# A delta-rule mixer joined from its projection to its scan, with the memory items woven into the feed-forward part

## The chip, the cores and the metric

The kernel runs on one core of a Trainium2 chip. The metric is the device time of one execution in microseconds; the median of three executions counts. Five things work beside one another: TensorE (PE, matmuls into eight PSUM banks), VectorE (DVE), ScalarE (ACT), GpSimd (POOL, idle here) and the DMA queue that SyncE (SP) feeds. They meet only at semaphores, and each runs its own list in order.

## The reference

Three blocks follow one another on x of 256 tokens by 1024 columns, in float32. The change touches the first one's first layer:

```python
x = x + 0.5 * swiglu(rms_norm(x, ffn1_norm[l]), ffn1_w_gu[l], ffn1_w_down[l])
h = rms_norm(x, mix_norm[l]) @ a_w_in[i]
qkv, gate, b_raw, a_raw, q_mem = jnp.split(h, ...)
o_a = gated_deltanet(qkv, gate, b_raw, a_raw, a_conv[i], a_A_log[i], a_dt_bias[i], a_out_norm[i])
o_m = memory_attention(q_mem, mem_n @ w_mem_kv[l])
x = x + jnp.concatenate([o_a, o_m], axis=-1) @ w_out[l]
```

gated_deltanet: silu of a causal convolution of four taps over qkv; q and k of each of the six heads divided by their length (`l2_norm`); beta = sigmoid(b_raw); g = -exp(A_log) * softplus(a_raw + dt_bias); per chunk of 64 tokens a triangular system from beta, k k^T and the decays exp(g_cum_i - g_cum_j), solved; then a scan over four chunks with a state of 128x128 per head; an RMS norm of the output and a factor silu(gate). The memory keys and values of both layers come from the normed 256 memory rows `mem_n`.

## The kernel before

Weights come as items of up to 1 MB (128 x 2048), in the order of `self.items`, through five slots. SyncE loads an item when its slot's last user is done (`load_weights`), ScalarE rounds it (`round_weights`, L210 and, with a gain, L214), VectorE takes the rest (`split_weights`, L227, L232), at most LEAD = 3 items ahead of TensorE, and TensorE makes three matmuls for each 128x128 block (hi*hi, hi*lo, lo*hi; L257 to L259 and L850 to L853). An item of 256 columns is 48 matmuls.

Each `K.stage` is a block; without `join` the one before is closed first, so that all engines end together. The order inside is written out by hand in one function per engine. Around the change:

- `ffn` (L813), eleven steps s: item a, item b, and the down item of the step before. An object `keys` can weave foreign items into step 0 and 1; only the latent part used it.
- `project_conv` (L1192), nine items: TensorE projects two chunks of 128 columns, VectorE scales them by the row norm into `conv_pad` (L1244), splits the next item, weighs the first tap (L1258) and adds three (L1264), ScalarE takes silu (L1229). ScalarE rounds without waiting for VectorE.
- `gates_and_memory` (L3356), nine items: three gate items, beta/a, q_mem, four memory items; the memory tokens are normed, transposed and rounded meanwhile.
- `group_norm` (L1381) on q and k: squares, 24 column sums, a root, its inverse spread to rows by matmuls with diagonals, q and k multiplied.
- transposes of k and v, the gates, `softplus` (L1446), `vector_chain`, the decays and products (L1570 to L1639), each in a stage of its own.
- the inverse (L1641 to L1717), two products, the scan (L1750 to L1806), `group_norm` of the output, `attend_memory`, `project_out`. The scan runs over four chunks: products with the state (L1768), new values (L1792), state growth (L1774), state update (L1801), outputs (L1779, L1780).

## Time and profile before

| | us |
|---|---|
| median of three executions | 3055.31 |
| lowest, highest | 3053.14, 3056.57 |
| the profiled execution | 3053.95 |
| its span in the profile | 3051.8 |
| TensorE busy | 2898.2 (95%) |
| VectorE busy | 1820.7 (60%) |
| ScalarE busy | 1457.3 (48%) |
| first feed-forward part | 29 to 217 |
| projection and convolution | 217 to 278 |
| gates and memory | 278 to 339 |
| norms of q and k | 339 to 361 |
| transposes, gates, softplus, decays, products | 361 to 402 |
| inverse, two products | 402 to 456 |
| scan | 456 to 502 |
| output norm, memory attention | 502 to 534 |

A timeline row gives start, length, engine, line, tiles and, in brackets, how long the engine had been idle and whom it waited for. Rows of one line that follow each other closely are merged (x6). Matmul lengths overlap; their pace is read from starts. A matmul of plain float32 operands shows as two records, so twelve of them are "x24".

### The profile page before, as it was taken

To read this page: it belongs to the slowest core of one execution; us is meant where nothing else is said; L and a number is where in the kernel's file an instruction comes from. 1 tells how busy PE (TensorE), PEld (TensorE's weight loads), DVE (VectorE), ACT (ScalarE), POOL (GpSimd) and SP (SyncE) were. 2 spreads that over 40 slices of the span, in tenths; PEclk is the share of its full clock that TensorE was granted. 3 is DMA by queue.
4 is the path that set the end of the run, shared out by engine and by line. 5 is a ranking of instruction groups with operands and counts; after the bars stand their busy time and mean duration, and the time that the engine had idled before them with its cause. 6 is when DMAs were issued, how large, how long until landed. Compare 5 with 4: busy or idle time off the path is not lost. (4 is left out here: it accounts for less than half of the span.)

```text
span 3051.8 us, 47640 instructions
## 1 busy us (share of the span) xinstructions
PE 2898.2 (95%) x20602; PEld 2688.5 (88%) x20602; DVE 1820.7 (60%) x2487; ACT 1457.3 (48%) x1927; POOL 16.3 (1%) x21
## 2 busy tenths in 40 slices
PE   6998788999999999999999898999999999999999
PEld 6998676899998799898999897998989899999898
DVE  5567473655656665545468756456556655656655
ACT  5554311545545554434466544445454544544543
POOL 0000000000000000000000200000000000000000
PEclk9999795999999899999999999999999999999999
DMA  6654200455554255555555254555555455554553
GB/s 199 193 180 156 80 1 0 159 187 170 176 190 160 85 193 187 173 193 166 169 166 179 79 170 164 183 178 165 193 182 177 149 184 193 179 187 146 200 188 130
DMA packets 370037, 489.16 MB, mean 160 GB/s; under 512 B 15183, under 2 KB 329124, under 8 KB 369700
## 3 DMA queue, kind: packets, MB, share of 16 engines
q1 hardware_dynamic: 369232, 485.90, 48.8%
q8 instruction: 163, 2.67, 0.4%
q14 instruction: 46, 0.38, 0.0%
q10 hardware_dynamic: 596, 0.21, 0.0%
HBM read 485.02 MB, written 1.05 MB: 159 GB/s over the span
## 5 line engine op out<-in xcount | busy, mean ns | idle before, releaser
L850 PE MATMUL work<-input_hi,weights_hi 128*128 128x256 f32 x3520 | 990.7, 281 | 8.2 <-DVE weights_lo L232 6.2
L853 PE MATMUL work<-input_hi,weights_lo 128*128 128x256 f32 x3520 | 987.1, 280 | 0.0
L852 PE MATMUL work<-input_lo,weights_hi 128*128 128x256 f32 x3520 | 987.1, 280 | 0.0
L227 DVE TENSOR_TENSOR weights_lo<-weights_raw,weights_hi 128x2048 fp32r<-128x2048 f32 (+1 forms) x282 | 629.5, 2236 | 376.2 <-ACT weights_hi L210 376.0
L850 PEld LDWEIGHTS work<-input_hi,weights_hi 128*128 128x128 f32 x3520 | 666.2, 189 | 13.8 <-DVE weights_lo L232 6.6
L852 PEld LDWEIGHTS work<-input_lo,weights_hi 128*128 128x128 f32 x3520 | 666.1, 189 | 4.4
L853 PEld LDWEIGHTS work<-input_hi,weights_lo 128*128 128x128 f32 x3520 | 665.9, 189 | 0.0
L214 ACT ACTIVATE weights_hi<-weights_raw,params 128x512 fp32r<-128x512 f32 (+2 forms) x736 | 462.0, 701 | 352.1 <-DMA weights_raw<-in_ffn_w_gu 176.2
L210 ACT ACTIVATE weights_hi<-weights_raw 128x2048 fp32r<-128x2048 f32 (+1 forms) x282 | 524.5, 1865 | 168.6 <-DMA weights_raw<-in_ffn_w_up 100.3
L232 DVE SCALAR_TENSOR_TENSOR weights_lo<-weights_raw,params,weights_hi 128x512 fp32r<-128x512 f32 (+2 forms) x736 | 492.7, 733 | 174.7 <-ACT weights_hi L214 174.6
L317 PE MATMUL acc<-weights_hi,hidden_hi 128*128 128x512 f32 x880 | 349.6, 397 | 6.3 <-DVE hidden_lo L952 5.0
L319 PE MATMUL acc<-weights_hi,hidden_lo 128*128 128x512 f32 x880 | 347.9, 395 | 0.0
L318 PE MATMUL acc<-weights_lo,hidden_hi 128*128 128x512 f32 x880 | 347.7, 395 | 0.0
L257 PE MATMUL work<-input_hi,weights_hi 128*128 128x256 f32 (+1 forms) x1008 | 287.7, 285 | 14.3 <-PEq L154 8.8
L258 PE MATMUL work<-input_lo,weights_hi 128*128 128x256 f32 (+1 forms) x1008 | 282.6, 280 | 0.0
L259 PE MATMUL work<-input_hi,weights_lo 128*128 128x256 f32 (+1 forms) x1008 | 282.3, 280 | 0.0
L941 DVE TENSOR_TENSOR gate_r<-work,inverse_root 128x512 f32<-128x512 f32 x88 | 60.8, 690 | 249.2 <-PE work L853 249.2
L257 PEld LDWEIGHTS work<-input_hi,weights_hi 128*128 128x128 f32 (+1 forms) x1008 | 189.3, 188 | 17.7 <-issue 15.3
L317 PEld LDWEIGHTS acc<-weights_hi,hidden_hi 128*128 128x128 f32 x880 | 166.1, 189 | 43.7 <-issue 8.8
L319 PEld LDWEIGHTS acc<-weights_hi,hidden_lo 128*128 128x128 f32 x880 | 166.1, 189 | 38.6
L915 ACT ACTIVATE hidden_hi<-hidden 128x512 fp32r<-128x512 f32 x110 | 69.4, 631 | 266.2 <-DVE hidden L949 266.2
L318 PEld LDWEIGHTS acc<-weights_lo,hidden_hi 128*128 128x128 f32 x880 | 166.4, 189 | 33.7
(518 smaller groups left out, 3408.8 us busy)
## 6 DMA issues: line engine op xcount, KB each, us to landing
weights_raw<-in_ffn_w_gu SPq DMA_DIRECT2D x176, 512.0 KB, 4.7
weights_raw<-in_ffn_w_in SPq DMA_DIRECT2D x176, 512.0 KB, 4.7
weights_raw<-in_ffn_w_down SPq DMA_DIRECT2D x66, 1024.0 KB, 4.9
weights_raw<-in_w_in SPq DMA_DIRECT2D x44, 1024.0 KB, 5.0
weights_raw<-in_ffn_w_out SPq DMA_DIRECT2D x44, 1024.0 KB, 4.8
weights_raw<-in_a_w_in SPq DMA_DIRECT2D x29, 1024.0 KB, 5.4
...
```

The costliest lines, as they stand in the source:

```text
L210: last = self.nc.scalar.activation(self.wh[:, n % SLOTS, 0:kc * cols], raw, ACT.Copy)
L214: last = self.nc.scalar.activation(hi[:, k, :], raw[:, k * cols:(k + 1) * cols], ACT.Copy, scale=g[:, gain[1] + k:gain[1] + k + 1])
L227: last = self.nc.vector.tensor_tensor(self.wl[:, n % SLOTS, 0:kc * cols], raw, self.wh[:, n % SLOTS, 0:kc * cols].bitcast(F32), ALU.subtract)
L232: last = self.nc.vector.scalar_tensor_tensor(out=lo[:, k, :], in0=raw[:, k * cols:(k + 1) * cols], scalar=g[:, gain[1] + k:gain[1] + k + 1 ...
L257: self.nc.tensor.matmul(o, wh[:, k, ms], hi[:, k, :], start=clear, stop=False, skip_group_check=True)
L258: self.nc.tensor.matmul(o, wh[:, k, ms], lo[:, k, :], start=False, stop=False, skip_group_check=True)
L317: self.nc.tensor.matmul(o, hi[:, k, ts], wh[:, k, cols], start=(first and k == 0), stop=False, skip_group_check=True)
L318: self.nc.tensor.matmul(o, hi[:, k, ts], wl[:, k, cols], start=False, stop=False, skip_group_check=True)
L319: last = self.nc.tensor.matmul(o, lo[:, k, ts], wh[:, k, cols], start=False, stop=(end and k == kc - 1), skip_group_check=True)
L850: nc.tensor.matmul(o, wh[:, k, ms], K.hi[:, c, :], start=(c == 0 and m == 0), stop=False, skip_group_check=True)
L852: nc.tensor.matmul(o, wh[:, k, ms], K.lo[:, c, :], start=False, stop=False, skip_group_check=True)
L853: last = nc.tensor.matmul(o, wl[:, k, ms], K.hi[:, c, :], start=False, stop=(c == DC - 1), skip_group_check=True)
```

## The change

The rest of the program stays as it is.

1. The four memory items move from behind the gates into step 1 of the first feed-forward part: class `MemoryKeys` is a second `keys` object. Its DMA of the memory tokens goes out at the start, its squares and root stand behind step 0 of ScalarE (`prepare`), its transposes in the middle of step 1, its four items behind it.
2. Projection, convolution, q_mem, norms, gates, transposes, decays and products are one joined stage of eleven items: beta/a first, then k, q, v, then q_mem. The first tap is weighed by ScalarE, beta comes from an exponential, the copies of k and v out of PSUM are ScalarE's.
3. q and k are not divided by their lengths any more. The inverse length of k enters as a column factor on the decays, on beta and on the scan's columns; that of q enters as a floor column in the output norm (`group_norm` loses its bias and gets one small VectorE operation).
4. The three gate items are projected inside the scan, half an item before and half behind the state growth of chunks 0 to 2; VectorE scales, ScalarE takes silu, and both prepare the items of `w_out` there.

```diff
@@ ffn @@
-    early, late = (2, NH // 2) if keys else (0, 0)
+    early, late = (keys.early, keys.late) if keys else (0, 0)
...
+                        keys.prepare(act)
@@ delta_mixer @@
-        project_conv(K, qkv, [K.g[f"conv_a{k}"] for k in range(4)], inp, norm=True)
-        gates_and_memory(K, gate, baT, qm)
...
+        chunk = lambda c: (NH, 0, 2 * NH)[c // 3] + 2 * (c % 3)
...
+        with K.stage(11, join=True) as (block, n0):
+            bank = lambda i: K.work[:, i % 3, :]
...
+                item(0)
+                feed.sum_row(pe)
+                item(1)
+                pe.wait_ge(*emptied(1))
...
+                item(2)
+                item(3)
+                item(4)
+                pe.wait_ge(*inputs(1))
+                sum_lengths(0)
+                item(5)
+                sum_lengths(1)
+                pe.wait_ge(*decay(1))
+                nc.tensor.matmul(K.work[:, 3, 0:N], K.c("tri64"), g, start=True, stop=True)
+                nc.tensor.matmul(K.work[:, 3, N:2 * N], K.c("same64"), g, start=True, stop=True).then_inc(*summed.up())
+                pe.wait_ge(*silued(3))
+                turn(0)
+                item(6)
+                feed.await_row(pe)
+                pe.wait_ge(*spread(1))
+                spread_rows(K.c("tri64"))
+                pe.wait_ge(*cumulated(1))
+                sum_lengths(2)
+                turn(1)
+                item(7)
+                pe.wait_ge(*rooted(1))
+                sum_lengths(3)
+                turn(2)
+                item(8)
+                pe.wait_ge(*decayed(1))
+                multiply(K.acc, kT)
+                sum_lengths(4)
+                item(9)
+                sum_lengths(5)
+                item(10)
+                pe.wait_ge(*masked_once(1))
+                pe.wait_ge(*spread(2))
+                spread_rows(K.c("ident"))
+                pe.wait_ge(*silued(9))
+                turn(3)
+                pe.wait_ge(*emptied(11))
+                multiply(K.work, qT)
+                turn(4)
+                turn(5)
...
+                def weigh_first_tap(c):
+                    if c >= 2:
+                        act.wait_ge(*silued(c - 1))
+                    act.wait_ge(*emptied(c + 2))
+                    for m in range(2):
+                        last = nc.scalar.activation(total[:, c % 2, m, :], pad[:, c % 2, m, 0:T], ACT.Copy,
+                                                    scale=taps[0][:, chunk(c) + m:chunk(c) + m + 1])
+                    last.then_inc(*first_tap.up())
+
+                def silu(c):
+                    act.wait_ge(*tap(6 * (c + 1)))
+                    nc.scalar.activation(qkv[:, chunk(c):chunk(c) + 2, :], total[:, c % 2, :, :], ACT.Silu).then_inc(*silued.up())
+                    if c < 6:
+                        act.wait_ge(*silued(c + 1))
+                        if c >= 2:
+                            act.wait_ge(*lengths(c - 1))
+                        nc.scalar.activation(sq[:, c % 2, :, :], qkv[:, chunk(c):chunk(c) + 2, :], ACT.Square).then_inc(*squared.up())
...
+                K.round_weights(act, n0 + LEAD)
+                feed.copy_row(act)
+                K.round_weights(act, n0 + 1 + LEAD)
+                for c in range(9):
+                    weigh_first_tap(c)
+                    K.round_weights(act, n0 + c + 2 + LEAD)
+                    if c == 6:
+                        act.wait_ge(*lengths(3))
+                        nc.scalar.activation(rk, K.work[:, 3, 2 * N:3 * N], ACT.Sqrt, bias=K.c("epsilon")[:, 0:1]).then_inc(*rooted.up())
+                        take(1)
+                    if c:
+                        silu(c - 1)
+                    if c == 1:
+                        act.wait_ge(*inputs(1))
+                        nc.scalar.activation(h_t(beta), ba[:, :, 0:NH].rearrange("p t h -> p h t"), ACT.Exp, scale=-1.0)
+                        nc.scalar.activation(al[:, 0, :], al[:, 0, :], ACT.Exp)
+                        nc.scalar.activation(e_, e_, ACT.Exp).then_inc(*exped.up())
...
+                    if c == 6:
+                        act.wait_ge(*clipped(1))
+                        nc.scalar.activation(E[:, :, :].rearrange("p n i -> p (n i)"), K.acc[:, 0:3, :].rearrange("p b i -> p (b i)"),
+                                             ACT.Exp)
+                        nc.scalar.activation(DT[:, :, :], DT[:, :, :], ACT.Exp).then_inc(*decayed.up())
...
+                def conv(c):
+                    dve.wait_ge(K.used, n0 + c + 2)
+                    if c >= 2:
+                        dve.wait_ge(*tap(6 * (c - 1)))
+                        dve.wait_ge(*first_tap(c - 1))
+                    nc.vector.tensor_tensor(pad[:, c % 2, :, 3:], two(bank(c + 1)), rstd(P, 2), ALU.mult).then_inc(*emptied.up())
+                    dve.wait_ge(*emptied(c + 2))
+                    K.split_weights(dve, n0 + c + 2 + LEAD)
+                    dve.wait_ge(*first_tap(c + 1))
+                    for k in range(1, 4):
+                        for m in range(2):
+                            y = total[:, c % 2, m, :]
+                            if k > 1:
+                                dve.wait_ge(*tap(6 * c + 2 * (k - 2) + m + 1))
+                            nc.vector.scalar_tensor_tensor(out=y, in0=pad[:, c % 2, m, k:k + T], scalar=taps[k][:, chunk(c) + m:chunk(c) + m + 1],
+                                                           in1=y, op0=ALU.mult, op1=ALU.add).then_inc(*tap.up())
...
+                conv(6)
+                dve.wait_ge(*rooted(1))
+                steps(lambda: nc.vector.reciprocal(rk, rk))
+                nc.vector.tensor_tensor(brk, beta, rk, ALU.mult).then_inc(*inverted.up())
+                dve.wait_ge(*decayed(1))
+                steps(lambda: nc.vector.tensor_tensor(DT[:, :, :], DT[:, :, :], row(rk), ALU.mult),
+                      lambda: nc.vector.tensor_tensor(AT[:, :, :], DT[:, :, :], K.c("upper64").unsqueeze(1).to_broadcast([P, N, P]), ALU.mult))
+                conv(7)
...
+                conv(8)
...
@@ delta_mixer @@
-        with K.stage() as (block, _):
+        with K.stage(3) as (block, n0):
...
+                K.round_weights(act, n0 + LEAD)
+                for i in range(3):
+                    act.wait_ge(*scaled(i + 1))
+                    nc.scalar.activation(gate[:, 2 * i:2 * i + 2, :], raw[:, i % 2, :, :], ACT.Silu).then_inc(*opened.up())
+                    K.round_weights(act, n0 + i + 1 + LEAD)
...
+                def gates(i, m):
+                    if m == 0 and i:
+                        pe.wait_ge(*scaled(i))
+                    K.project_part(pe, n0 + i, K.acc[:, 3, :], (K.hi, K.lo), m)
...
                         last.then_inc(*ws.up())
+                    if c < C - 1:
+                        gates(c, 0)
                     pe.wait_ge(*newv(c + 1))
                     if c < C - 1:
                         for hh in range(NH):
                             last = nc.tensor.matmul(six(2, hh), ktok[r, NT * hh + t, :], vnew[r, hh, :],
                                                     start=True, stop=True)
                         last.then_inc(*grown.up())
+                        gates(c, 1)
...
+                K.split_weights(dve, n0 + LEAD)
...
+                        dve.wait_ge(K.used, n0 + c + 1)
+                        if c == 2:
+                            dve.wait_ge(*opened(1))
+                        nc.vector.tensor_tensor(raw[:, c % 2, :, :], K.acc[:, 3, :].rearrange("p (m t) -> p m t", m=2),
+                                                K.rstd[:, 0:T].unsqueeze(1).to_broadcast([P, 2, T]), ALU.mult).then_inc(*scaled.up())
+                        K.split_weights(dve, n0 + c + 1 + LEAD)
@@ MemoryKeys @@
+class MemoryKeys:
+    early, late = 0, 4
...
+    def sum_squares(self, pe):
+        K = self.K
+        for j in range(4):
+            t, half = j // 2, j % 2
+            pe.wait_ge(*self.normed(t + 1))
+            for c in range(4):
+                at = half * 512 + c * P
+                last = K.nc.tensor.transpose(K.acc[:, j, c * P:(c + 1) * P], self.mem[:, t, at:at + P], K.c("ident"))
+            last.then_inc(*self.turned.up())
+
+    def expand(self, pe, n):
+        K, nc = self.K, self.K.nc
+        pe.wait_ge(*self.split(4))
...
+        pe.wait_ge(*self.passed(4))
...
@@ build @@
-        plan_ffn(K, gu[0], gu[0], 0, FF, dn[0], "ffn1_0")
+        def memory_items(s):
+            if s == 1:
+                for c in (0, MH * MD):
+                    for layer in range(2):
+                        plan_columns(K, A["w_mem_kv"][layer], c, MH * MD)
+        plan_ffn(K, gu[0], gu[0], 0, FF, dn[0], "ffn1_0", memory_items)
         AW = NH * DK
-        plan_columns(K, A["a_w_in"][0], 0, 4 * AW)
-        plan_columns(K, A["a_w_in"][0], 4 * AW, 2 * NH)
-        plan_columns(K, A["a_w_in"][0], 4 * AW + 2 * NH, MH * MD)
-        for c in (0, MH * MD):
-            for layer in range(2):
-                plan_columns(K, A["w_mem_kv"][layer], c, MH * MD)
+        for c, n in ((4 * AW, 2 * NH), (AW, AW), (0, AW), (2 * AW, AW), (4 * AW + 2 * NH, MH * MD), (3 * AW, AW)):
+            plan_columns(K, A["a_w_in"][0], c, n)
...
-        ffn(K, first, FeedTail(K, mix), join=True)
+            mix, second = mixer(K.g["mix_0"]), next_ffn()
+            ffn(K, first, FeedTail(K, mix), join=True, keys=MemoryKeys(K, K.ctx2))
```

How the lists move. VectorE at the second convolution turn, before:

```order
L1244 TENSOR_TENSOR conv_pad<-work,inverse_root 128x2x256 [waits weights_used]
L227 TENSOR_TENSOR weights_lo<-weights_raw,weights_hi 128x2048 [waits weights_rounded]
L1258 TENSOR_SCALAR conv_sum<-conv_pad,params 128x256 [waits conv_raw_ready]
L1258 TENSOR_SCALAR conv_sum<-conv_pad,params 128x256
L1264 SCALAR_TENSOR_TENSOR conv_sum<-conv_pad,params,conv_sum 128x256 [waits conv_tap_added] x6
```

and now:

```order
L1474 TENSOR_TENSOR gate<-work,inverse_root 128x2x256 [waits weights_used]
L227 TENSOR_TENSOR weights_lo<-weights_raw,weights_hi 128x2048 [waits weights_rounded,projection_scaled]
L1483 SCALAR_TENSOR_TENSOR h<-gate,params,h 128x256 [waits conv_raw_ready]
L1483 SCALAR_TENSOR_TENSOR h<-gate,params,h 128x256
L1483 SCALAR_TENSOR_TENSOR h<-gate,params,h 128x256 [waits conv_tap_added] x4
L1505 TENSOR_SCALAR delta_small<-delta_small 128x12 [waits gates_exponentials]
```

The pad now lies in the tile of the gates and the sums in h. The first tap has left the list, the split waits for the rounding as before, and small gate operations (L1505 and its followers) stand behind the turn.

ScalarE at the first turns, before:

```order
L210 ACTIVATE weights_hi<-weights_raw 128x2048 [waits weights_landed_2]
L1229 ACT_TABLE_LOAD
L1229 ACTIVATE qkv<-conv_sum 128x512 [waits conv_tap_added]
L210 ACTIVATE weights_hi<-weights_raw 128x2048 [waits weights_landed_3]
L1229 ACTIVATE qkv<-conv_sum 128x512 [waits conv_tap_added]
```

and now:

```order
L1394 ACTIVATE h<-gate,params 128x256 [waits projection_scaled]
L1394 ACTIVATE h<-gate,params 128x256
L210 ACTIVATE weights_hi<-weights_raw 128x2048 [waits weights_landed_2]
L1400 ACT_TABLE_LOAD
L1400 ACTIVATE qkv<-h 128x512 [waits conv_tap_added]
L1405 ACTIVATE h<-qkv 128x512 [waits conv_silued]
L1434 ACT_TABLE_LOAD
L1434 ACTIVATE delta_small<-beta_a_raw 128x12 [waits gates_ready]
L1435 ACTIVATE a_log_bias<-a_log_bias 128x6
L1436 ACTIVATE delta_small<-delta_small 128x12
L1394 ACTIVATE h<-gate,params 128x256 [waits projection_scaled,conv_silued]
L1394 ACTIVATE h<-gate,params 128x256
```

The rounding (L210) stood in front of the silu of the turn before and waited for its landing alone; now it stands behind the first tap (L1394), which waits for the scaled pad, and table loads stand between silu and the exponentials.

TensorE in the scan, before, where one chunk's state products are followed by its state growth:

```order
L1768 MATMUL work<-delta_wide_39,delta_wide_42 64x128 [waits scan_state] x6
L1774 MATMUL work<-qkv,k_tokens 128x128 [waits scan_values]
L1774 MATMUL work<-qkv,k_tokens 128x128 x5
L1779 MATMUL acc<-qkv,delta_wide_39 128x64
L1780 MATMUL acc<-delta_wide_43,qkv 128x64
```

and now:

```order
L1710 MATMUL work<-delta_wide_36,delta_wide_39 64x128 [waits scan_state] x6
L288 MATMUL acc<-input_hi,weights_hi 128x256 [waits weights_split,projection_scaled]
L289 MATMUL acc<-input_lo,weights_hi 128x256
L290 MATMUL acc<-input_hi,weights_lo 128x256
...
L1718 MATMUL work<-qkv,k_tokens 128x128 [waits scan_values]
L1718 MATMUL work<-qkv,k_tokens 128x128 x5
L288 MATMUL acc<-input_hi,weights_hi 128x256
```

Between the products with the state (L1710) and the state growth (L1718) now lie 24 matmuls of a gate item (L288 to L290), and 24 more behind the growth.

## Rows read from the trace of the kernel before

**Rows 1.** The page, clock granted to TensorE in 40 slices of 76.3 us.

```profile
PEclk9999795999999899999999999999999999999999
```

**Rows 2.** Stretches: length, busy time and count by engine, clock, DMA share, GB/s.

```profile
53.00:219.00 166.00, 165.64 (x1158) 153.37 (x1157) 96.70 (x122) 80.53 (x110) 0.00 (x0) 1.00 0.59 186
...
217.00:278.00 61.00, 52.65 (x442) 52.01 (x440) 56.98 (x104) 28.86 (x34) 0.00 (x0) 0.97 0.51 161
278.00:339.00 61.00, 55.33 (x424) 54.39 (x424) 26.94 (x33) 28.55 (x40) 0.00 (x0) 0.89 0.47 156
339.00:361.00 22.00, 17.57 (x60) 11.39 (x60) 8.24 (x13) 5.35 (x9) 0.00 (x0) 0.69 0.15 48
361.00:402.00 41.00, 20.79 (x126) 19.52 (x126) 23.45 (x46) 9.12 (x12) 0.00 (x0) 0.77 0.01 1
...
456.00:502.00 46.00, 40.30 (x156) 34.23 (x156) 9.73 (x23) 0.00 (x0) 0.00 (x0) 0.53 0.00 0
```

**Rows 3.** Timeline (start, length, engine, line, tiles, idle before): two marks.

```profile
224.55 0.47 PE L257 MATMUL work<-input_hi,weights_hi 128*128 128x256 f32 x1
...
402.12 1.29 DVE L1688 TENSOR_TENSOR qkv<-delta_wide,const 128x512 f32<-128x512 f32 x2 [0.32 <-PEq L154]
```

**Rows 4.** Timeline rows and two stretches of TensorE, behind the feed-forward terms.

```profile
45.44 0.63 ACT L915 ACTIVATE hidden_hi<-hidden 128x512 fp32r<-128x512 f32 x1 [2.16 <-DVE hidden L949]
...
298.22 1.91 PE L3389 MATMUL acc<-const,mem_tokens 128*128 128x128 f32 x16
...
288.48 1.05 ACT L3417 ACTIVATE mem_lo<-mem_tokens 128x1024 fp32r<-128x1024 f32 x1
...
290.68 1.28 ACT L3420 ACT_TABLE_LOAD   x1
291.97 0.30 ACT L3420 ACTIVATE mem_columns<-mem_columns,const 128x2 f32<-128x2 f32 x1
...
279.00:284.00 5.00, 5.00 (x24) 0.50 0.66 210
...
320.00:330.00 10.00, 10.00 (x86) 1.00 0.51 159
```

**Rows 5.** Timeline: one convolution turn on VectorE, and ScalarE's rounding and scaling.

```profile
249.34 0.70 DVE L1244 TENSOR_TENSOR conv_pad<-work,inverse_root 128x512 f32<-128x512 f32 x1
249.94 2.29 DVE L227 TENSOR_TENSOR weights_lo<-weights_raw,weights_hi 128x2048 fp32r<-128x2048 f32 x1
...
252.66 2.48 DVE L1264 SCALAR_TENSOR_TENSOR conv_sum<-conv_pad,params,conv_sum 128x256 f32<-128x256 f32 x6
...
250.00 1.90 ACT L210 ACTIVATE weights_hi<-weights_raw 128x2048 fp32r<-128x2048 f32 x1
...
746.74 3.29 ACT L214 ACTIVATE weights_hi<-weights_raw,params 128x256 fp32r<-128x256 f32 x8
```

**Rows 6.** Timeline: pieces between the turns.

```profile
371.35 0.17 DVE L1468 TENSOR_TENSOR delta_small<-delta_small 128x12 f32<-128x12 f32 x1
...
379.88 3.19 DVE L1607 TENSOR_SCALAR delta_wide<-acc,delta_small 128x128 f32<-128x128 f32 x12 [4.86 <-PE acc L1577]
...
386.03 1.76 DVE L1611 TENSOR_TENSOR delta_wide<-delta_wide,const 128x1536 f32<-128x1536 f32 x1 [2.09 <-ACT delta_wide L1639]
...
383.18 1.45 ACT L1637 ACTIVATE delta_wide<-acc 128x1536 f32<-128x1536 f32 x1 [7.80 <-DVE delta_wide L1607]
```

**Rows 7.** Timeline of TensorE: twelve products of 128x128, low and high clock.

```profile
402.87 5.01 PE L1667 MATMUL work<-const,qkv 128*128 128x128 f32 x24 [5.19 <-DVE qkv L1688]
...
451.45 2.84 PE L1738 MATMUL work<-h,delta_wide 128*128 128x128 f32 x24
```

**Rows 8.** Timeline of TensorE in the scan.

```profile
478.54 2.93 PE L1774 MATMUL work<-qkv,k_tokens 64*128 64x128 f32 x12 [1.04 <-DVE qkv L1792]
481.39 0.69 PE L1779 MATMUL acc<-qkv 128*128 128x64 f32 x2
482.01 0.69 PE L1780 MATMUL acc<-delta_wide,qkv 64*128 64x64 f32 x2
```

724 lines of the change are left out of this document (250 added, 474 removed).

## The prediction

> **What bounds the kernel now.** I read the 40 slices first for the place: TensorE's clock falls below 9 tenths in two places, the fifth and the seventh slice (305 to 381 and 458 to 534 us) [rows 1], and both lie in the first mixer. Then the busy times by stage [rows 2]. The feed-forward stretch 53 to 219 us has TensorE busy for 165.64 of 166.00 us, so work added there is paid in full. The mixer is different. 217 to 278 us (projection and convolution) has VectorE busy 56.98 of 61; TensorE ends its nine weight items near 270 and then stands. 278 to 339 (gates, memory) is TensorE again, 55.33 of 61. 339 to 361 and 361 to 402 (norms, transposes, softplus, decays) use no weights at all, move 48 and 1 GB/s, and have TensorE busy 17.57 of 22 and 20.79 of 41, at a mean clock of 0.69 and 0.77: they are a string of short hand-overs. 456 to 502 (scan) has TensorE busy 40.30 of 46 at a clock of 0.53, that is nearly all at the lower level, 1.2 GHz. So there are some 63 us of latency-bound work between 339 and 402 that can slip between weight items, and that is what the change tries to use.
>
> I work in three pieces, in the times of the profiled execution: the feed-forward part, the joined stage (from 224.55 us, when the first convolution item starts, to the first mask of the inverse at 402.12 [rows 3]), and the scan.
>
> **Feed-forward part, +31.2.** Four memory items move in, 48 matmuls each. At full clock 86 matmuls of 256 columns lie in 10 us, 0.116 to 0.117 each [rows 4], so an item is 5.6 and four are 22.4. The sixteen transposes cost 1.9 [rows 4]. Nothing hides them, because TensorE is full there. Then three waits. (1) Today the down item of step 0 starts at 53.01, so step 1's first weight item ends one item earlier, at 47.4; now the transposes stand behind it and need the scaled memory tokens. ScalarE starts on these only when its hidden_hi copy ends, 45.44 + 0.63 = 46.1 [rows 4]. From there the two squares run until the table load (288.48 to 290.68, 2.2), the load takes 1.28 and the root 0.30 [rows 4]: 49.9. VectorE's reciprocal and the first scaling take another 0.9, so TensorE waits from 47.4 to 50.8: 3.4. (2) After an idle stretch like that the clock comes back late: at 279 to 284 us 24 matmuls ran in 5.0 us at 0.50 [rows 4] where 2.8 would do. I take 2.5; bounds 0 and 5. (3) TensorE waits once for the accumulators to be copied out before the down item. A copy of that size takes ScalarE 0.63 (hidden_hi [rows 4]), and with two hand-overs I take 0.9. Sum 22.4 + 1.9 + 3.4 + 2.5 + 0.9 = 31.1, and 0.1 of hand-overs. The memory tokens' own DMA (1 MB) is queued behind the first five weight items and is wanted 30 us later: nothing.
>
> **Joined stage, -72.7.** The number that decides is the time of one convolution turn on VectorE. Before, ScalarE rounded an item a whole turn ahead, so VectorE never waited: scale, split, eight taps, one behind the other: 0.6 + 2.2 + 0.5 + 2.4 = 5.7 [rows 5]. In the new order ScalarE waits for the scaled pad, weighs the first tap, and only then rounds the item that VectorE wants to split next. So each turn is a serial chain: pad 0.69 and a hand-over, 0.72; two activations of 128x256 with a scale column at 0.41 each, 0.82 (eight took 3.29); rounding 1.90 and hand-over, 1.93; split 2.20; six taps 2.38 [rows 5]. That is 8.05 instead of 5.70, although VectorE has two instructions fewer. TensorE needs 5.6 and is no longer the last. Nine turns: 72.5. Between the turns VectorE does, in order:
> - after turns 0, 1, 2 and 4: 5, 8, 3 and 3 small operations, 0.17 plus a hand-over each [rows 6], 0.2 taken: 4.0 (the exponentials and the logarithm of ScalarE are ready just in time);
> - after turn 5: twelve clips, 3.2 [rows 6]; and the wait of turn 6 for its item, because TensorE stands behind the transposes for ScalarE's copy, loses its clock and does that item in nearly 8: 2.0 taken, bounds 0 and 3;
> - after turn 6: two small ones, 0.4, then the wait for the exponentials. ScalarE does after its rounding: table load, root, copy, table load, silu, square, table load, two exponentials, 1.28 + 0.21 + 0.60 + 1.28 + 0.63 + 0.63 + 1.28 + 1.45 + 1.45 = 8.8 (loads, silu and exponentials [rows 4, 6]); VectorE needs 5.0 for split, taps and the two small ones, so it waits 3.8. Then two products of 1.76 [rows 6]: 7.7 in all;
> - after turn 7: one product, 1.8; after turn 8: q_mem 0.7, three products 5.3, small ones 0.6, and 1.4 for the last value transposes, their copies and the stage's end: 8.0.
>
> Sum 72.5 + 4.0 + 5.2 + 7.7 + 1.8 + 8.0 = 99.2. The first turn starts when the first convolution item is done, 224.55 + 5.6 + 0.1 = 230.3. The inverse then starts at 329.5 instead of 402.12: -72.6. (The beta/a item of 24 matmuls takes the place of the first one's second half in front of the row sum; nothing is won or lost before 224.55.) The gates item and the small matmuls of TensorE (two spreads and two products of twelve at 2.84 [rows 7], transposes, lengths) lie in the 2.4 us that it has spare in each turn. What covers them is exactly the slow hand-over; without it they would be on the path.
>
> A page of the Trainium skill speaks against this part (ScalarE: Activation LUTs, "What ACT_TABLE_LOAD costs"): a switch of table costs the load and a drain of about 1.38 us behind it. The rows show the root starting at 291.97, 1.29 after the load began at 290.68, with no drain [rows 4]. By the page, turn 6's three switches would add 4.1 and those of turns 1 and 2 about 3; the time would be some 7 us more. I go by the row.
>
> **Inverse, -2.1.** Its first twelve products ran at the low clock, 5.01, against 2.84 for as many at the high one [rows 7]. TensorE now comes from dense work, with a gap of some 3 us.
>
> **Scan, +5.9.** Per chunk now, at the low clock: products with the state 2.9 and state growth 2.93, 24 passes of output, 7.4 (a pair follows another every 0.62: 481.39 and 482.01), and a wait of 1.04 for VectorE [rows 8]; 14.1. Each of three chunks gets one gate item, half before the wait and half behind the growth: 5.6 at full clock, 10.1 at half (24 matmuls in 5.0 [rows 4]). Those halves are dense, so the clock rises: with everything at the high clock a chunk is 1.4 + 2.8 + 1.5 + 2.8 + 3.7 = 12.2. New on VectorE: at the start a split waits for ScalarE's rounding, which delays the first values by 4.5 (1.93 + 2.29 + hand-overs), to 460.7; TensorE waits 2.2 of it behind its first half item. Later the chain scale 0.69, silu 0.63, rounding 1.90, split 2.29 stands in front of the next values, 5.7 against 5.1 of outputs and products: just covered by the next half item of 2.8. Walk: first chunk ends 467.0; second 479.9 (a wait of 0.7); then outputs and state products are thin work, the clock falls at about 480 and returns in the next gate halves, so the third ends 494.5; the last state products 497.3, values 498.4, outputs at half clock 505.9, final copy 507.8, against 501.9 today. Bounds: all high 500.8; all low 532.5. Out norm: one more small operation in its chain, +0.4.
>
> **Sum**: 31.2 - 72.6 - 2.1 + 5.9 + 0.4 = -37.2. The profiled execution took 3053.95 (span 3051.8), the median of three is 3055.31, so 3016.8 by the one and 3018.1 by the other. I say 3017.
>
> **Rivals.**
> 1. *TensorE-bound joined stage.* If the hand-over is not on the path (ScalarE far enough ahead), TensorE's work decides: 10 items 56, spreads and products 11.5, transposes 3, lengths about 5 (the 339 to 361 stretch holds twice as much and more in 17.57 [rows 2]), small ones 0.6, tail 3: 79, ending at 304 to 307 instead of 329.5. That gives 2993 to 2996. Against it: the wait stands in front of the rounding in every turn. 0.10.
> 2. *The scan stays at 1.2 GHz.* For it: the whole scan is there today (0.53) [rows 2]. Against: after the idle stretch before 279 the clock was back when 5 us of weight matmuls had run [rows 4], and each chunk now has more than that. Then the scan ends at 532.5: 3017 + 24.7 = 3042. 0.16.
> 3. *Slower than before: the clock stays low in joined stage and scan.* TensorE now stands 2.4 us in each turn. If that holds the clock down, an item is 10.2, longer than the 8.05 of the turn, and TensorE's 77 us become about 145: the stage ends near 372 and its gain shrinks to 30, which the feed-forward part's 31 eats; with the scan's 30 the kernel would be at about 3084. It decides as soon as items take over 8.05, since then they are the longest link. The page TensorE: Matmul & The Clock Gate of the Trainium skill ("HAM oscillation — how this bites in real kernels") says that bursts separated by waits restart at half clock each time. Against it, from rows: an item at half clock leaves no gap at all, and after the 5.0 us of such matmuls at 279 to 284 the next ones ran at full clock [rows 4]. 0.04.
> 4. *It does not do what it says*, the stages merely change places: within 0.2%. 0.02.
>
> **How the numbers follow.** My forecast has 0.68, its own range 3005 to 3030 (stage +-8, feed-forward part -5 to +3, scan -7 to +5). With rival 2 that is 0.84 up to 3043; rival 1 mostly falls below. Range 3000 to 3043. A difference under about 0.2% (6 us) can't be told from none. Faster 0.94, same 0.02, slower 0.04.
>
> **What the changed profile would show.** A VectorE turn of 8 us in which the split waits for ScalarE's weights_hi (wrong if 5.7); TensorE waiting about 3.4 us before the memory transposes near 50 us; ten ScalarE table loads inside the joined stage, three of them in turn 6; the inverse starting 41 us earlier than today (about 361); a scan of 50 to 54 us whose clock is over 0.7. The prediction is wrong if the scan's clock stays at 0.5, or if TensorE's items in the joined stage run at half clock.

## The result and the profile after

The changed kernel takes **3023.61 us** (median of 4 runs, 3016.28 to 3027.38) against 3054.22 before (4 runs): ratio 0.9903, 95 % interval 0.9890 to 0.9915. The forecast was 3017, range 3000 to 3043. A second measurement of the same two kernels gave 3017.37 against 3051.75, ratio 0.9888 (0.9875 to 0.9902).

The page's clock row, as [rows 1]:

```profile
PEclk9999896999999999999999999999999999999999
```

The two low places of before, the fifth and the seventh slice, are still there, but shallower: 8 and 6 tenths where it was 7 and 5. Stretches of the changed kernel (columns as in [rows 2]), in the order of the rows: feed-forward part from step 0's second weight item to the first down item (the memory items lie in it), joined stage, inverse with the products behind it, scan, output norm and attention.

```profile
35.80:83.80 48.00, 43.77 (x354) 43.13 (x352) 30.27 (x44) 32.05 (x51) 0.00 (x0) 0.96 0.48 154
...
261.90:361.30 99.40, 79.21 (x606) 77.79 (x606) 65.69 (x116) 58.03 (x78) 0.00 (x0) 0.88 0.34 106
361.30:413.00 51.70, 48.53 (x408) 47.64 (x408) 37.89 (x55) 8.96 (x15) 0.00 (x0) 0.97 0.00 1
413.00:469.50 56.50, 49.54 (x300) 44.21 (x300) 22.03 (x31) 10.66 (x8) 0.00 (x0) 0.81 0.18 56
469.50:504.40 34.90, 25.91 (x79) 15.32 (x79) 17.85 (x42) 12.47 (x31) 0.00 (x0) 0.58 0.00 0
```

With marks that exist in both traces, as in [rows 3], the whole difference up to the first matmul of the output projection can be laid out (us):

| stretch | before | after | difference | forecast |
|---|---|---|---|---|
| to the first convolution item | 224.55 | 255.93 | +31.4 | +31.2 |
| from there to the inverse's first mask | 177.57 | 105.36 | -72.2 | -72.6 |
| inverse and the products behind it | 52.17 | 51.69 | -0.5 | -2.1 |
| from there to the scan's final copy | 47.64 | 56.48 | +8.8 | +5.9 |
| output norm, attention | 33.71 | 34.93 | +1.2 | +0.4 |
| sum | 535.64 | 504.39 | **-31.3** | -37.2 |
| everything behind | 2516.1 | 2521.0 | +4.9 | 0 |

The last line is no effect of the change. The same work there took 2508.4 us in the second profile of the same kernel, and 2511.0 to 2517.5 in the others of this study. In that second profile the output projection starts at 504.51. So -31 is what the change does, and the medians (-30.6 and -34.4) scatter around it.

How the joined stage runs is seen in one plain turn. Timeline of VectorE (start, length, line, tiles, idle before and what ended it):

```profile
289.56 0.69 DVE L1474 TENSOR_TENSOR gate<-work,inverse_root 128x512 f32<-128x512 f32 x1
293.15 2.29 DVE L227 TENSOR_TENSOR weights_lo<-weights_raw,weights_hi 128x2048 fp32r<-128x2048 f32 x1 [2.90 <-ACT weights_hi L210]
295.36 2.46 DVE L1483 SCALAR_TENSOR_TENSOR h<-gate,params,h 128x256 f32<-128x256 f32 x6
297.74 0.69 DVE L1474 TENSOR_TENSOR gate<-work,inverse_root 128x512 f32<-128x512 f32 x1
```

ScalarE in the same turn:

```profile
290.35 0.91 ACT L1394 ACTIVATE h<-gate,params 128x256 f32<-128x256 f32 x2 [1.86 <-DVE gate L1474]
291.16 1.89 ACT L210 ACTIVATE weights_hi<-weights_raw 128x2048 fp32r<-128x2048 f32 x1
293.07 1.28 ACT L1400 ACT_TABLE_LOAD   x1
294.36 0.63 ACT L1400 ACTIVATE qkv<-h 128x512 f32<-128x512 f32 x1
```

Read the two together: pad, then first tap on ScalarE, then rounding on ScalarE, then split, then taps. Each link starts when the one before ends, 8.18 us from pad to pad. What VectorE waited for in the whole stage (us in total, times, longest):

```profile
DVE weights_lo L227 <- ACT weights_hi L210: 26.1, 9, 2.9
DVE delta_wide L1537 <- ACT delta_wide L1452: 3.7, 1, 3.7
DVE gate L1474 <- PE work L259: 2.7, 2, 1.6
```

The first row is the hand-over of nine turns, the second the exponentials in turn 6, and TensorE is waited for only 2.7 us in all.

### The profile page after: what moved, and what is told of

Read it like the earlier page. It is cut to its first block and busy times, and to the rows that moved or that the text cites. A ratio compares the mean times of both kernels' runs of the same rounds, so it can differ in the third digit from the quotient of the medians.

```text
span 3025.5 us, 47569 instructions
## 1 busy us (share of the span) xinstructions
PE 2878.8 (95%) x20590; PEld 2673.7 (88%) x20590; DVE 1803.6 (60%) x2454; ACT 1477.2 (49%) x1966; POOL 16.3 (1%) x21
## 5 line engine op out<-in xcount | busy, mean ns | idle before, releaser
L227 DVE TENSOR_TENSOR weights_lo<-weights_raw,weights_hi 128x2048 fp32r<-128x2048 f32 (+2 forms) x282 | 629.6, 2236 | 406.6 <-ACT weights_hi L210 406.4
L210 ACT ACTIVATE weights_hi<-weights_raw 128x2048 fp32r<-128x2048 f32 (+2 forms) x282 | 524.1, 1864 | 178.1 <-DMA weights_raw<-in_ffn_w_up 108.0
L257 PE MATMUL work<-input_hi,weights_hi 128*128 128x256 f32 (+1 forms) x960 | 276.2, 288 | 6.9 <-DVE weights_lo L227 4.0
L258 PE MATMUL work<-input_lo,weights_hi 128*128 128x256 f32 (+1 forms) x960 | 270.5, 282 | 0.0
L259 PE MATMUL work<-input_hi,weights_lo 128*128 128x256 f32 (+1 forms) x960 | 270.4, 282 | 0.0
L257 PEld LDWEIGHTS work<-input_hi,weights_hi 128*128 128x128 f32 (+1 forms) x960 | 182.1, 190 | 10.3 <-issue 6.4
```

What stands on the lines that cost most here:

```text
L210: last = self.nc.scalar.activation(self.wh[:, n % SLOTS, 0:kc * cols], raw, ACT.Copy)
L227: last = self.nc.vector.tensor_tensor(self.wl[:, n % SLOTS, 0:kc * cols], raw, self.wh[:, n % SLOTS, 0:kc * cols].bitcast(F32), ALU.subtract)
L257: self.nc.tensor.matmul(o, wh[:, k, ms], hi[:, k, :], start=clear, stop=False, skip_group_check=True)
L258: self.nc.tensor.matmul(o, wh[:, k, ms], lo[:, k, :], start=False, stop=False, skip_group_check=True)
```

## Experiments

All numbers in "measured" are of the run named. The changed kernel itself had medians of 3023.61 and 3017.37, so the total of a single edit (3013 to 3023 in most cases) says little by itself; what an edit did is read from marks in its trace. The stage is counted from the first convolution pad to the first mask of the inverse (99.37 us in the changed kernel).

### Rounding ahead of the first tap

```
 for c in range(9):
-    weigh_first_tap(c)
     K.round_weights(act, n0 + c + 2 + LEAD)
+    weigh_first_tap(c)
```

> The changed kernel with one edit: in ScalarE's loop over the nine convolution turns the rounding of the next weight item stands ahead of the first tap (it stood behind it). In the trace of the changed kernel a turn is a serial chain of 8.2 us: pad 0.69, first tap 0.91, rounding 1.90, split 2.29, taps 2.46. Theory (serial hand-over): with the rounding done in the turn before, VectorE goes from the pad straight to the split while ScalarE weighs the tap: 0.69 + 2.29 + 2.46 = 5.4, less than the 5.9 of TensorE's item, so TensorE becomes the longest: ten and a half items 62, spreads and products 12, the rest 9 to 12: the inverse starts near 340 instead of 361.3, time 3002 us (2996 to 3010), and a turn shows VectorE waiting for TensorE. Rival A (ScalarE's own work of a turn, with its table loads 5.4 to 7.1 and some 11 in turn 6, is next): turns 1, 2 and 6 stay at 7 to 10 us, inverse at 346 to 352, time 3008 to 3015. Rival B (the order doesn't matter): 3021 to 3026.

Measured: **3002.96 us** (ratio to before 0.9828, 0.9812 to 0.9844). A plain turn is 5.8 to 5.9. Timeline of VectorE:

```profile
290.89 0.68 DVE L1474 TENSOR_TENSOR gate<-work,inverse_root 128x512 f32<-128x512 f32 x1
291.61 2.29 DVE L227 TENSOR_TENSOR weights_lo<-weights_raw,weights_hi 128x2048 fp32r<-128x2048 f32 x1
293.82 2.46 DVE L1483 SCALAR_TENSOR_TENSOR h<-gate,params,h 128x256 f32<-128x256 f32 x6
```

The split follows the pad without a wait. Waits of VectorE in the stage:

```profile
DVE gate L1474 <- PE work L259: 5.5, 3, 3.0
DVE delta_wide L1537 <- ACT delta_wide L1452: 4.8, 1, 4.8
...
DVE weights_lo L227 <- ACT weights_hi L210: 0.7, 1, 0.7
```

26.1 us of waiting for rounded weights have become 0.7. The stage is 82.3, 17.1 less. That is less than expected: laid on the changed kernel's times the inverse starts at 344.2 (340 foreseen), because turns 5 and 6 stay at 11.5 and 14.1. The total of 3003 came out as expected all the same, which is partly luck: some 2 us of it are the scan's (below). That TensorE would become the longest link of a plain turn did not come true: VectorE waits for it only at the first pad and ahead of turns 6 and 8, and the plain turns are VectorE's own work but for one wait of 0.67. ScalarE did nothing new. The rounding's data lay ready all along; it stood in ScalarE's queue behind an instruction that waited for VectorE. The Trainium skill (Perfetto Trace Analysis, "Tensor Engine Instruction (MATMUL, LD_WEIGHTS)") notes that ScalarE and VectorE are strict first-in, first-out; the run agrees.

### Half of TensorE's work in the stage

```
-    K.project(pe, n0 + i, bank(i), ...)
+    K.project(pe, n0 + i, bank(i), ..., half=i > 0)    # k in range(kc // 2)
```

The kernel leaves out half of the rows of ten weight items, so its output is not that of the changed kernel; only its time is of use.

> The changed kernel with the ten weight items of the joined stage behind the beta/a item projected over half of their rows only (24 matmuls instead of 48 each, the output leaves that half out): TensorE loses 240 matmuls, 29 us of its work. Theory (the serial hand-over over ScalarE sets the turn): only what TensorE itself is waited for goes, the first item (2.9) and the 1.6 us before turn 6; against it stand small matmuls at a lower clock (2 to 3 us). The turns stay at 8.2, the wait of 3.7 for the exponentials stays, time 3021 (3016 to 3025). Rival (TensorE is the bound of the stage): 25 us less, 2998.

Measured: 3013.2 us (0.9876, 0.9858 to 0.9894). The window of the stage, and what VectorE waits for in it:

```profile
260.40:359.60 99.20, 60.50 (x378) 58.65 (x376) 65.54 (x116) 58.01 (x78) 0.00 (x0) 0.74 0.33 105
```

```profile
DVE weights_lo L227 <- ACT weights_hi L210: 26.4, 10, 2.9
DVE delta_wide L1540 <- ACT delta_wide L1455: 3.7, 1, 3.7
```

With 240 matmuls fewer the stage is 99.20 instead of 99.37. Turn by turn, pad to pad: 9.04, 9.86, 8.70, 8.17, 8.69, 11.28, 15.91, 9.85 against 9.06, 9.88, 8.70, 8.18, 8.68, 12.97, 15.92, 9.85. Only turn 5 lost its wait for the item. TensorE's busy time fell by 18.7 us (79.2 to 60.5), not by the 28 that 240 matmuls take at full clock, since more of its work ran at the lower clock (mean 0.74 in the stage, 0.88 with full items). TensorE is not the bound: the first rival falls. The time was 8 us lower than expected, and 4 under the changed kernel's second median. That is not the stage: against the changed kernel's first profile 5.4 us of it are the scan, at another clock (below). Of the 2.9 us by which the first item is shorter only 1.5 arrived, since VectorE was still splitting. The Trainium skill says that bursts of matmuls separated by waits restart at half clock each time (TensorE: Matmul & The Clock Gate, "HAM oscillation — how this bites in real kernels"). For long waits this run agrees: the work behind each of TensorE's six waits of 3.5 to 8.4 us in the stage ran at half clock. Behind the shorter waits of this study the clock went either way (below).

### Exponentials first, then the root too

The first edit moves `E` and `DT` ahead of the first tap of turn 6, the second also the root and the copy of the turned keys:

```
 for c in range(9):
+    if c == 6:
+        act.wait_ge(*lengths(3)); activation(rk, ..., ACT.Sqrt); take(1)   # second edit only
+        act.wait_ge(*clipped(1)); activation(E, ..., ACT.Exp); activation(DT, ..., ACT.Exp)
     weigh_first_tap(c)
```

> The changed kernel with one edit: in turn 6 ScalarE does the two exponentials of the decays ahead of the first tap instead of behind root, copy, silu and square. In the trace of the changed kernel VectorE clips until 317.79, ScalarE is idle from 313.2 to 320.2 with the exponential's table loaded, and later VectorE waits 3.7 us (328.0 to 331.7) for the exponentials behind three table loads. Theory: the exponentials run 317.8 to 320.8, the first tap is 0.7 later, the wait of 3.7 goes: the inverse starts 3.0 earlier, 358.3, time 3020.6. With the two table loads that become one the result can be 0.3 better. Rival (what is late next takes it: root and the sixth item of TensorE): the wait of VectorE shows up at another instruction of turns 6 and 7 and the inverse stays within 1 us of 361.3.

Measured: 3022.89 us (0.9894, 0.9879 to 0.9910), stage 98.57, only 0.8 less. Waits of VectorE, then of TensorE, in the stage:

```profile
DVE weights_lo L227 <- ACT weights_hi L210: 26.1, 9, 2.9
DVE gate L1474 <- PE work L259: 5.8, 3, 2.5
```

```profile
PE work L1313 <- ACT delta_small L1433: 5.2, 1, 5.2
```

The rival holds. The wait of 3.7 is gone, and VectorE waits 2.5 for TensorE's item instead, because TensorE stood 5.2 us for the root, which still waits behind first tap and rounding. (It stood as long in the changed kernel, where the wait for the exponentials hid it.)

> The changed kernel with one edit more than the one that put the exponentials first: in turn 6 ScalarE does the root of the lengths and the copy of the turned keys as well ahead of the first tap. With the exponentials alone moved, TensorE still stood 5.16 us (321.7 to 326.9) for the root behind first tap and rounding, its item came late, and VectorE waited 2.5 us for that item where it had waited 3.7 for the exponentials. Theory (root and exponentials both wait behind the rounding): TensorE passes straight from the sixth item to the seventh, turn 6 is 8.2 + 0.4 + 3.5 and 0.7 for the later first tap, 12.8 instead of 15.9, the inverse starts 3 us earlier than in the changed kernel, time 3020.6. Rival (the wait moves again): turn 6 stays above 14.5, time 3022.5 or more.

Measured: 3015.65 us (0.9878, 0.9862 to 0.9895). Turn 6 is 12.11, stage 96.83: 2.5 less than in the changed kernel, near the 3 expected. Waits of TensorE:

```profile
PE acc L1329 <- ACT delta_wide L1456: 4.9, 1, 4.9
PE acc L1323 <- ACT qkv L1400: 4.3, 1, 4.3
```

The root is no longer among them. TensorE now runs ahead and stands 4.9 later, for the copy that turn 8 makes, where it costs nothing but clock. Again the time says more than the stage: it is 8 us under the changed kernel's first median, with 5.3 of it in the scan, but only 1.7 under the second.

### First values ahead of the split

```
 def _(dve):
-    K.split_weights(dve, n0 + LEAD)
     ...
     nc.vector.tensor_copy(vnew[r], Uh[r, t]).then_inc(*newv.up())
+    K.split_weights(dve, n0 + LEAD)
```

> The changed kernel with one edit: at the start of the scan VectorE copies the first values before it splits the waiting weight item (it split first, and had to wait for ScalarE's rounding). In the trace of the changed kernel the values came at 419.45, 4.5 us late, but TensorE had its first half gate item to do until 417.83, so it waited 1.68. Theory (only what TensorE waits counts): growth starts at 417.8 instead of 419.5, and the low clock of 420.6 to 424.0 goes with the wait: the scan (first gate matmul to final copy, 54.7 us) becomes 51.5 to 53, time 2 to 3 us less than the 3023.6 of the changed kernel: 3021. Rival (the delay of 4.5 is on the path in full): 3019. Rival (the wait moves to the next hand-over, since the split now stands between values and state): no change of the scan, 3023.6.

Measured: 3019.88 us (0.9890, 0.9874 to 0.9906). The changed kernel's waits of TensorE in the scan were:

```profile
PE acc L288 <- PEq L154: 1.8, 1, 1.8
PE work L1718 <- DVE qkv L1735: 1.7, 1, 1.7
PE acc L1724 <- DVE qkv L1738: 1.1, 1, 1.1
PE work L1718 <- DVE qkv L1738: 0.6, 1, 0.6
```

Here the second is gone and the others stand. In the window of the scan (52.9 us long) TensorE is idle 5.21 us instead of 6.96: 1.75 gained, as TensorE's own wait said. The scan is 3.5 shorter; the other 1.8 is clock.

### Gates behind the scan

The calls `gates(c, 0)` and `gates(c, 1)` move out of the chunk loop of TensorE, and VectorE's scale and split with them, behind the last outputs.

> The changed kernel with the three gate items taken out of the scan's chunks and projected in one piece behind the last outputs. Theory (half of the gate work is hidden in the scan): the scan is as in the kernel before, 45.8 us, plus the 4.5 us by which the split delays the first values, now in full, and the three items behind it take 17.7 at full clock and about 3 more until the clock is back and for the last hand-over: 71 instead of 54.7, time 3038 (3034 to 3042). Rival (weaving hides nothing; gate work costs the same wherever it stands): 3024. Rival (the gate matmuls in the scan also keep its clock up, without them all of it is low as before): that is part of the 45.8; a scan of over 52 us before the gates would speak for something else.

Measured: 3041.82 us (0.9969, 0.9957 to 0.9982). Scan, then gate items:

```profile
412.90:464.00 51.10, 41.46 (x165) 35.71 (x166) 13.07 (x25) 3.36 (x2) 0.00 (x0) 0.58 0.00 0
464.00:483.10 19.10, 17.52 (x137) 16.90 (x136) 5.97 (x4) 4.88 (x4) 0.00 (x0) 0.95 0.32 111
```

The last gate matmul ends 70.2 us after the stage before, as expected (71); scaling, rounding and splitting of the next item behind it take another 5.5. The output norm starts 24.9 us after the last copy of the scan, where it was 0.3 with the gates woven in. The scan without gates takes 51.1 at a clock of 0.58. With the gates in it, it took 51.0 to 56.5 at 0.92 to 0.81. So the dense halves pay most of their own time by the clock at which the thin products beside them then run: 0 to 5.4 us for work that costs 24.6 behind the scan. Not all of that is the clock, though. Without the first gate half TensorE stands 6.5 us for the late first values instead of 1.7, and it idles 9.6 us in the window instead of 7.0. Against the scan of the kernel before, whose first values were not late (47.6), the woven gates cost 3.4 to 8.8.

### Memory root before the hidden copy

```
+    if s == 0: keys.prepare(act)      # squares and root
     act.wait_ge(*hidden(s + 1))       # then hidden_hi
```

and on VectorE `keys.scale(dve)` ahead of hidden_lo.

> The changed kernel with one edit: in step 0 of the first feed-forward part the squares and the root of the memory tokens run on ScalarE before it copies hidden_hi, and VectorE scales the tokens before hidden_lo (both stood behind). In the trace of the changed kernel ScalarE idles 43.1 to 45.2, the root is ready at 49.56 and TensorE waits 3.23 us (47.37 to 50.60), after which its clock is low for one stretch of 3.4 us (51.97 to 55.39). Theory: root ready at 46.85, first scaled half at 47.8, TensorE waits 0.4; with the wait the low stretch goes too (1.7 us): the later parts start 4 to 5 us earlier, time 3019. Rival (the low clock has another cause, the sixteen transposes): only 2.8 gained, 3020.8, and the clock still falls near 52. Rival (what is late next, the split of the following weight item): gain under 1.

Measured: 3020.26 us (0.9894, 0.9878 to 0.9911). TensorE's waits from step 0's second weight item to the first down item, in the changed kernel:

```profile
PE acc L1803 <- DVE mem_tokens L1839: 3.2, 1, 3.2
PE acc L257 <- DVE mem_lo L1863: 0.3, 1, 0.3
```

and here, with the window:

```profile
PE acc L257 <- DVE mem_lo L1869: 2.4, 1, 2.4
PE acc L1809 <- DVE mem_tokens L1845: 0.4, 1, 0.4
```

```profile
36.70:82.60 45.90, 42.35 (x354) 41.70 (x352) 29.40 (x43) 31.95 (x51) 0.00 (x0) 1.00 0.48 161
```

The wait fell to 0.4 and the clock rose to full (0.96 before), as expected; but 2.4 came back at the next hand-over, mem_lo, which VectorE made behind two splits. 2.2 us gained where 4 to 5 were foreseen.

That the low stretch went because the wait went is not shown. Two kernels with this part unchanged kept the wait and had no low stretch. Transposes and first memory matmul in the changed kernel, then in the one with half items:

```profile
50.60 2.41 PE L1803 MATMUL acc<-const,mem_tokens 128*128 128x128 f32 x16 [3.23 <-DVE mem_tokens L1839]
60.08 0.39 PE L257 MATMUL acc<-mem_hi,weights_hi 128*128 128x256 f32 x1 [0.33 <-DVE mem_lo L1863]
...
50.51 1.97 PE L1806 MATMUL acc<-const,mem_tokens 128*128 128x128 f32 x16 [3.25 <-DVE mem_tokens L1842]
59.99 0.39 PE L259 MATMUL acc<-mem_hi,weights_hi 128*128 128x256 f32 x1 [1.91 <-DVE mem_lo L1866]
```

In both the memory items begin 9.48 us after the transposes. At half clock TensorE is busy until mem_lo is there, at full clock (1.00 from 50 to 64 us) it waits 1.9 for it. So the low stretch cost nothing here: VectorE's list, reciprocal, scaling, two splits, mem_lo, sets the time, and this is also why making mem_lo late took back a part of the gain.

### Together, and two more edits

> The changed kernel with four edits together: rounding ahead of the first tap, root and exponentials ahead of turn 6, first values ahead of the split in the scan, memory root ahead of the hidden copy. Measured so far: rounding first 3003, values first 3.7 less, memory root early 2.2 less in the feed-forward part (a new wait of 2.4 for mem_lo took the rest). Theory (the parts are independent, and turn 6, 14.1 with the rounding first, becomes 10 to 11 without the root's and exponentials' wait): 3003 - 3.7 - 2.2 - 4 = 2993 (2988 to 2997). Rival (with the rounding first TensorE is the bound also in turn 6, so moving ScalarE's work gains nothing): 2997. Rival (the low clock comes back at another place): 3000.

Measured: **2991.24 us** (0.9801, 0.9787 to 0.9816), stage 75.8. VectorE's waits for rounded weights and TensorE's items are 5.9 us in all, for the exponentials of the decays none.

The next edit makes mem_hi and mem_lo ahead of the second of the two weight items:

> The kernel with all four edits (2991.2) and a fifth: in step 1 of the first feed-forward part ScalarE and VectorE make the memory tokens' halves (mem_hi, mem_lo) ahead of the second of two weight items, which TensorE wants 12 us later. In its trace TensorE stands 2.42 us (56.38 to 58.80) for mem_lo behind two splits. Theory: mem_lo is ready 2.3 us earlier, TensorE waits under 0.3, time 2.3 less: 2989 (2986 to 2992). Rival (what is late next, the postponed weight item): the wait moves to the memory items and the time stays at 2991.

Measured: **2988.30 us** (0.9787, 0.9774 to 0.9801), 63 us less than before, where the changed kernel measured beside it had 34. TensorE's waits in the feed-forward stretch:

```profile
PE acc L1811 <- DVE mem_tokens L1847: 0.5, 1, 0.5
PE acc L257 <- DVE mem_lo L1871: 0.2, 1, 0.2
```

The stretch is 43.5 us instead of 48.0, and 45.7 with four edits.

The last edit puts each half gate item of the scan one place later, first on top of the kernel with the first values ahead of the split, then on top of the kernel with five edits:

> The kernel with the first values ahead of the split (3019.9), and in it the six gate halves of the scan one place later: none ahead of the first values, the last one ahead of the last values, where TensorE waited 1.05 us. The work is the same. In the trace of that kernel the clock stays low from 453.2 to 497.6, from the outputs of the third chunk on, and the last outputs take 7.5 us instead of 3.7. Theory (the clock follows dense work with some delay, so the low stretch only moves): the wait of 1.05 is filled, the clock falls one step later, but the last half itself or the outputs before it run low: scan (last product of the stage before to final copy, 56.0 there) within 2 us of that, time 3019 (3016 to 3022). Rival (the half brings the last outputs to full clock): 3 to 4 us less, 3016. Rival (a half at the low clock costs 5.6 where 3 was): 2 to 3 more, 3022.5.

Measured: 3017.06 us (0.9886, 0.9873 to 0.9900); scan 51.2 instead of 52.9.

> All edits together: the kernel with five edits (2988.3), and in its scan the six gate halves one place later. Alone, against the kernel with the values first, that move brought the start of the output projection 3.0 us forward (from the first convolution pad, 239.1 to 236.1): last outputs 4.33 instead of 7.48, last half 4.31 instead of 3.1, no wait before the last values. Theory (where the clock falls in the scan decides, and a dense half right before the last outputs keeps it up): the same 3 us here, 2985.5 (2983 to 2989). Rival (the gain came from where the low stretches happened to lie): anywhere from no gain to 1 us slower, 2988 to 2989, with the last outputs at 7.5 again.

Measured: 2989.59 us (0.9795, 0.9781 to 0.9808), no better than without it. The scan is 51.0 where it was 54.6, but TensorE idles 5.34 in it against 5.30 (alone 5.42 against 5.21): no wait was won. The kernel with four edits, whose scan code is that of the one with five, had shown 51.9. By the total the rival comes nearest. But its sign, last outputs at 7.5 again, did not show: they took 4.32 us in both kernels with this edit, as the theory wanted, and 5.3 to 7.5 in all others. The output projection starts 1.7 us earlier than in the kernel with five edits (472.2, 473.9), although the feed-forward part and the joined stage, the same code in both, took 3.6 longer. What the edit is worth, anything from nothing to 3.6 us, can't be told from where the clock happens to fall.

### The changed kernel once more

> The changed kernel as it is, once more. Six traces with the same inverse and scan code (changed kernel, rounding first, exponentials first, memory root early, half items, root first) have 106.4, 104.0, 105.4, 104.7, 101.5 and 100.6 us from the first mask to the final copy, while the turns of the joined stage agree to 0.02 us. Theory (the granted clock in the scan falls at other places from run to run, the order of the work does nothing to it): this run again shows the same turns, first feed-forward part and joined stage within 1.5 us, and a stretch of 100 to 106.5 whose difference sits in the matmul durations, not in waits. Rival (each kernel has its own fixed pattern): 106.4 within 0.3. Time 3022 (3018 to 3025).

Measured: 3017.37 us. The turns agree to 0.02 us but for one at 13.07 (12.97). From first mask to final copy 106.21 us against 106.41: within the rival's 0.3, so this run can't tell the two. Across kernels the picture is plain, though. Windows of the scan, all with the same instructions in it:

| kernel | window | TensorE busy | idle | clock |
|---|---|---|---|---|
| changed | 56.5 | 49.54 | 6.96 | 0.81 |
| changed, once more | 56.4 | 49.38 | 7.02 | 0.81 |
| memory root early | 55.1 | 48.22 | 6.88 | 0.83 |
| exponentials first | 55.0 | 48.03 | 6.97 | 0.83 |
| rounding first | 54.3 | 47.45 | 6.85 | 0.86 |
| root first | 51.1 | 44.23 | 6.87 | 0.92 |
| half items | 51.0 | 44.11 | 6.89 | 0.92 |

TensorE's idle time is the same to 0.2 us in all seven. The 5.4 us between them are matmuls at one clock or the other. Row of the kernel with the root first, to be laid beside the changed kernel's row at the top:

```profile
411.40:462.50 51.10, 44.23 (x300) 39.82 (x300) 22.00 (x31) 10.64 (x8) 0.00 (x0) 0.92 0.19 62
```

What puts the low stretches in one place or another is open: the same kernel gave the same place twice, kernels that reach the scan at another moment gave another. No run set that moment on purpose. The order of the work alone does not fix it. The instructions up to 60 us are the same in nine profiles, with a wait of 3.1 to 3.3 us for the scaled memory tokens in each; a low stretch lay behind it in seven of them and none in two.

## Why the forecast was right, and where it was off

**The feed-forward part** came out at +31.4 for +31.2. TensorE waited 3.23 for the scaled tokens (3.4). Some 1.8 us went to matmuls at half clock behind that (2.5), the items took 23.1 instead of 22.4 (0.120 per matmul instead of 0.117), the two waits for accumulators and mem_lo 1.0 (0.9). The agreement to 0.2 is partly luck, in two ways. The term for the clock had the right size but was not what held TensorE: where the clock stayed up, TensorE waited 1.9 for mem_lo instead and the stretch took the same 48.0 to 48.2 us. The forecast had no wait for mem_lo. And in the nine profiles with this part unchanged the first convolution item starts anywhere from 255.6 to 258.6.

**The joined stage** was the step on which all hung, and its mechanism is shown from both sides: halving TensorE's work left it at 99.2, moving one rounding took 17. Term by term, from the pads' starts:

| term | forecast | measured |
|---|---|---|
| nine turns | 9 x 8.05 = 72.5 | 9 x 8.18 = 73.6 |
| small operations after turns 0, 1, 2, 4 | 4.0 | 3.6 |
| after turn 5: clips and wait | 5.2 | 4.8 (wait 1.59) |
| after turn 6 | 7.7 | 7.7 (wait 3.73) |
| after turn 7 | 1.8 | 1.7 |
| after turn 8 | 8.0 | 8.0 |
| sum | 99.2 | 99.4 |

(The 19 small operations at 0.2 add to 3.8; the forecast wrote 4.0.) Link by link, from start to start in the turn shown above: pad to first tap 0.79 (0.72 forecast), first tap to rounding 0.81 (0.82), rounding to split 1.99 (1.93), split to taps 2.21 (2.20), taps to pad 2.38 (2.38). So the two hand-overs between VectorE and ScalarE were taken 0.07 and 0.06 too short, and the rest was right. The first tap's row of 0.91 overlaps the start of the rounding. The forecast also gave TensorE 2.4 us to spare in each turn. It took its spare time otherwise: it ran ahead and then stood in a few waits, the longest of 4.8, 4.0 and 5.2 us, and the granted clock was at half in three stretches, 291 to 301, 311 to 315 and 322 to 332 us. The forecast had named weight items at half clock in this stage as a sign of being wrong. A quarter of the stage ran so, and except for 1.59 us before turn 6 VectorE's turns didn't feel it. Turn 6 had its three table loads, and none had a drain behind it. Timeline of ScalarE there:

```profile
322.90 1.28 ACT L1428 ACT_TABLE_LOAD   x1
324.19 0.27 ACT L1428 ACTIVATE delta_small<-work,const 128x12 f32<-128x12 f32 x1
324.36 0.59 ACT L1410 ACTIVATE k_tokens<-acc 128x512 f32<-128x512 f32 x1
324.97 1.28 ACT L1400 ACT_TABLE_LOAD   x1
326.26 0.63 ACT L1400 ACTIVATE qkv<-h 128x512 f32<-128x512 f32 x1
...
327.57 1.28 ACT L1450 ACT_TABLE_LOAD   x1
328.87 1.45 ACT L1450 ACTIVATE delta_wide<-acc 128x1536 f32<-128x1536 f32 x1
```

0.01 to 0.02 us lie between each load and the function behind it. So the row of before was the right one to go by. The drain that the Trainium skill adds to a load (ScalarE: Activation LUTs, "What ACT_TABLE_LOAD costs") doesn't show behind it, nor ahead of it: the rounding before the first load ended at 322.88, 0.02 us earlier.

**The inverse** gained 0.5, not 2.1. The step that failed is "TensorE now comes from dense work, with a gap of some 3 us", and with it the counting of 5.01 - 2.84 in full. TensorE came from the stage at full clock, with gaps of 1.2 and 2.2 us and 0.7 us of transposes between them, and the clock still fell. Timeline of TensorE:

```profile
362.04 4.62 PE L1589 MATMUL work<-const,qkv 128*128 128x128 f32 x24 [2.23 <-DVE qkv L1610]
```

Its first twelve products took 4.62 instead of the 2.84 of [rows 7]. Before they took 5.01. The gap alone doesn't decide it: it was 2.23 or 2.24 in all thirteen profiles with the joined stage, and in one, with the memory root early, the clock stayed at 1.00:

```profile
362.85 2.05 PE L1595 MATMUL work<-const,qkv 128*128 128x128 f32 x16 [2.23 <-DVE qkv L1616]
365.48 1.13 PE L1595 MATMUL work<-const,qkv 128*128 128x128 f32 x8 [0.58 <-DVE h L1626]
```

Even there inverse and products took 51.25 us, 0.9 less than before and not 2.1, because at full clock TensorE waits longer for VectorE between the products (0.58 here). So more than half of the term was never to be had.

**The scan** cost 8.8, not 5.9. The first values came 4.5 late and TensorE waited 1.7 of it (2.2 foreseen), so the walk's waits were right; each of the three chunks took 0.8 to 1.5 longer than walked, with parts at half clock where the walk had full. The term was a single number for something that the same code does in 51.0 to 56.5 us, +3.4 to +8.8 by this sum. My 5.9 lies inside, and the range of -7 to +5 around it covered both ends. The scan took 54.7 us from its first gate matmul at a clock of 0.81; I had said 50 to 54 and over 0.7, so its length lies just outside. (The low-clock chunk of 14.1 in the forecast is the period in the trace; the terms listed for it add to 14.3.) Rival 2 (clock stays at 0.5) and rival 3 (low in stage and scan) fall with that. Rival 1 did not hold for this kernel, but the edits brought it near: from its first convolution item the stage takes 88 us with the rounding ahead, and 80 to 82 with turn 6 freed as well; 79 by that rival.

**Output norm and attention** cost 1.2 instead of 0.4: the norm's chain is 1.0 longer, of which the added small operation is 0.14 (from the last copy to the reciprocal), and the rest is clock: the last two spreading products took 2.07 instead of 1.12. The five misses, 0.2 + 0.4 + 1.6 + 2.9 + 0.8, add to the 6 us between -37.2 and -31.3. What the medians differ by beyond that is the scatter of everything behind the mixer.
